# Rotation partners: four SBUF to SBUF transfers in place of a permutation product

## What is computed

```python
def apply_rope_2(x, cos, sin):
    x1, x2 = jnp.split(x32, 2, axis=-1)
    return jnp.concatenate([x1 * c - x2 * s, x2 * c + x1 * s], axis=-1)

def axial_rope_2(x, row_cs, col_cs):
    return jnp.concatenate([apply_rope_2(x[..., :half], *row_cs),
                            apply_rope_2(x[..., half:], *col_cs)], axis=-1)
...
qa = axial_rope_2(rms(qa, q_norm_a[l]), row_cs, col_cs)      # 8 query heads
ka = axial_rope_2(rms(ka, k_norm_a[l]), row_cs, col_cs)      # 2 key heads
y_a = gqa_attention(qa, ka, va) @ w_branch_a[l]
for g in range(3):                                           # 3 dilated groups, 4 heads
    qs.append(apply_rope_2(rms(qb, q_norm_b[l, g]), *seq_cs))
    kss.append(apply_rope_2(rms(kb, k_norm_b[l, g]), *seq_cs))
y_b = dilated_attention(qs, kss, vs) @ w_branch_b[l]
```

## Time and profile before

| | |
|---|---|
| median of 3 runs | 3612.27 us (3611.25 to 3614.24) |
| the profiled execution | 3599.83 us, span 3598.0 us |
| TensorE busy | 3462.9 us, 96% of the span |
| VectorE busy | 2141.8 us, 60% |
| ScalarE busy | 1230.7 us, 34% |
| GpSimd busy | 332.7 us, 9% |
| TensorE's granted clock, mean | 0.988 |
| chain that ended last | TensorE 52%, issue 32%, VectorE 11%, ScalarE 4% |
| DMA | 359.58 MB, mean 100 GB/s |

### The profile page before, as it was taken

One profiled execution on the slowest core, in us unless ns is written; L12 is line 12 of the kernel. 1 busy time (PEld: TensorE's weight loads), 2 busy tenths in 40 slices (PEclk: granted clock), 3 DMA queues, 4 the chain that ended last, 5 costly groups with the idle time before them and its releaser, 6 DMA issues.

```text
span 3598.0 us, 45143 instructions
## 1 busy us (share of the span) xinstructions
PE 3462.9 (96%) x17184; PEld 2724.0 (76%) x17184; DVE 2141.8 (60%) x2850; ACT 1230.7 (34%) x1526; POOL 332.7 (9%) x334
## 2 busy tenths in 40 slices
PE   7999999999999998999998999999999999999999
PEld 3677768888888676678886477878888577878887
DVE  6457558666666465576667566366667665355443
ACT  1235435112213355342225333342223433333222
POOL 0000102001002000010003010011001010001000
PEclk9999999999999998999999999999999999999999
DMA  8221202322232122034442011234443011222222
GB/s 337 82 78 53 75 0 83 128 106 93 97 125 90 57 77 74 21 141 164 163 163 78 31 66 54 88 124 169 163 163 135 32 66 47 82 106 94 93 94 105
DMA packets 52252, 359.58 MB, mean 100 GB/s; under 512 B 5960, under 2 KB 6600, under 8 KB 11024
## 3 DMA queue, kind: packets, MB, share of 16 engines
q1 hardware_dynamic: 35744, 256.92, 20.2%
q10 hardware_dynamic: 16368, 100.73, 7.6%
HBM read 355.31 MB, written 2.32 MB: 99 GB/s over the span
## 4 chain that ended last, share of the span: by engine, by line
PE 52%; issue 32%; DVE 11%; ACT 4%; DMA 1%; POOL 1%; DVEq 0%; ACTq 0%; POOLq 0%
PE pair L548 21%; PE pair L1045 11%; PE pair L616 3%; DVE arena L2190 2%; PE pair L1115 2%; PE pair L586 2%; PE pair L719 1%; PE pair L878 1%; DVE w_lo L2105 1%; PE pair L560 1%; PE pair L967 1%; ACT w_hi L1399 1%; PE pair L1187 1%; PE pair L942 1%; DVE arena L2465 1%
## 5 line engine op out<-in xcount | busy, mean ns | idle before, releaser
L2105 DVE TENSOR_TENSOR w_lo<-raw,w_hi 128x2048 fp32r<-128x2048 f32 x221 | 506.9, 2294 | 263.8 <-ACT w_hi L1399 258.1
L1399 ACT ACTIVATE w_hi<-raw 128x2048 fp32r<-128x2048 f32 x221 | 421.6, 1908 | 661.1 <-PE pair L548 608.5
L548 PE MATMUL pair<-h_hi,w_hi 128*128 128x512 f32 (+2 forms) x1856 | 597.4, 364 | 5.7 <-DVEq L2087 2.7
L548 PE MATMUL pair<-h_hi,w_lo 128*128 128x512 f32 (+2 forms) x1856 | 594.5, 362 | 0.0
L548 PE MATMUL pair<-h_lo,w_hi 128*128 128x512 f32 (+2 forms) x1856 | 594.3, 362 | 0.0
L548 PE MATMUL pair<-u_hi,w_hi 128*128 128x512 f32 (+3 forms) x1152 | 388.4, 373 | 10.2 <-DVE x L2146 5.8
L2190 DVE SCALAR_TENSOR_TENSOR arena<-arena,cact 128x256 f32<-128x256 f32 x756 | 375.7, 520 | 19.5
L548 PE MATMUL pair<-u_hi,w_lo 128*128 128x512 f32 (+3 forms) x1152 | 381.9, 368 | 0.0
L548 PE MATMUL pair<-u_lo,w_hi 128*128 128x512 f32 (+3 forms) x1152 | 381.2, 367 | 0.0
L548 PEld LDWEIGHTS pair<-h_hi,w_hi 128*128 128x128 f32 (+2 forms) x1856 | 309.1, 183 | 67.4 <-issue 7.3
L548 PEld LDWEIGHTS pair<-h_hi,w_lo 128*128 128x128 f32 (+2 forms) x1856 | 308.9, 183 | 62.3
(11 more groups left out here) (359 smaller groups left out, 4961.7 us busy)
## 6 DMA issues: line engine op xcount, KB each, us to landing
raw<-in_wt_dram SPq DMA_DIRECT2D x222, 1024.0 KB, 4.8
arena<-in_modw_dram ACTq DMA_DIRECT2D x78, 1024.0 KB, 4.9
arena<-in_modw_dram SPq DMA_DIRECT2D x18, 1024.0 KB, 7.2
arena<-negm_rows_dram ACTq DMA_DIRECT2D x16, 384.0 KB, 4.3
arena<-in_fconst_dram ACTq DMA_DIRECT2D x2, 2688.0 KB, 9.8
x<-in_xt_dram SPq DMA_DIRECT2D x1, 3072.0 KB, 16.4
arena<-in_brope_dram ACTq DMA_DIRECT2D x4, 640.0 KB, 3.9
out_dram<-x SPq DMA_DIRECT2D x1, 2048.0 KB, 7.2
```

Of the source, the lines that this page charges most:

```text
L548: mm = pe.matmul(pp[p][0:m, lo:hi], a[0:rows, k * width + c0:k * width + c0 + m], b[0:rows, k, lo:hi], start=(k == 0 and i == 0), stop=(k ...
L1399: act.activation(w_hi[slot][:], raw[slot][:], ACT.Copy).then_inc(w_hi_done, 1)
L2105: dve.tensor_tensor(w_lo[slot][:], raw[slot][:], w_hi[slot][:].bitcast(F32), ALU.subtract)\
```

## The change

The permutation product (L1055) is gone. Instead ScalarE, behind the two reads of a rotation, waits for its own scaling and issues four transfers of 32 rows x 512 (64 KB each) from qg to a new buffer qs, which swap the two blocks of 32 rows within each 64. VectorE waits for all four (64 on a semaphore of the rotation's parity) and multiplies qs by the sine from SBUF, where it read bank 3. So that the partner is always 32 rows away, the host puts the columns of the grouped queries and keys, their gains and the tables in another order; the part of the table where the permutation was is loaded as zeros. The scaling signals the semaphore `rope_gained` in place of `act_pool`; GpSimd waits for that.

```diff
+        rope_gained = sem("rope_gained")
+        rope_partner = [sem(f"rope_partner_in{i}") for i in range(2)]
-        b_perm = area(0, P)
+        g_qs = [area(GR0 + 16 * S + i * S, S) for i in range(2)]
+        r_qs = [area(R0 + (13 + i) * S, S) for i in range(2)]
...
-            def bank_rope(slot, sq, qg):
+            def bank_rope(slot, sq):
                 pair_read(slot)
                 take_pair(2)
                 pe.matmul(bank(2), b_blk, sq, start=True, stop=True).then_inc(job_act, 1)
-                take_pair(3)
-                pe.matmul(bank(3), b_perm, qg, start=True, stop=True).then_inc(job_dve, 1)
...
+            def partner(i, qs, qg):
+                act.wait_ge(rope_gained, t.next(rope_gained))
+                for at in range(0, P, 64):
+                    for a, b in ((at, at + 32), (at + 32, at)):
+                        act.dma_start(qs[a:a + 32, :], qg[b:b + 32, :]).then_inc(rope_partner[i], 16)
+
-            def rope_scaled(slot, col, qg, sq):
+            def rope_scaled(slot, col, i, qg, sq, qs):
                 act.wait_ge(rope_done, t.next(rope_done))
-                act.activation(qg, bank(slot), ACT.Copy, scale=prm[:, col:col + 1]).then_inc(act_pool, 1)
+                act.activation(qg, bank(slot), ACT.Copy, scale=prm[:, col:col + 1]).then_inc(rope_gained, 1)
                 act.activation(sq, bank(slot), ACT.Square).then_inc(pair_free[slot], 1)
+                partner(i, qs, qg)
...
-                                   scale=prm[:, col:col + 1]).then_inc(act_pool, 1)
+                                   scale=prm[:, col:col + 1]).then_inc(rope_gained, 1)
                     act.activation(g_sq[i], late_y[i], ACT.Square, bias=bias[:, i, 0:1]).then_inc(pair_free[i], 1)
+                    partner(i, g_qs[i], g_qg[i])
...
-            def bank_rope(tm, qc, root, hi, lo, source, back):
-                job()
-                finish(dve.tensor_tensor(tm, bank(3), b_sin, ALU.mult), pair_free[3])
+            def bank_rope(tm, i, qs, qc, root, hi, lo, source, back):
+                dve.wait_ge(rope_partner[i], t.next(rope_partner[i], 64))
+                finish(dve.tensor_tensor(tm, qs, b_sin, ALU.mult))
...
-                    pool.wait_ge(act_pool, t.next(act_pool))
+                    pool.wait_ge(rope_gained, t.next(rope_gained))
...
-        w = a["w_in_2"][l]
+        w = a["w_in_2"][l][:, _turned_columns()]
...
+def _turned_head():
+    return np.arange(64).reshape(2, 2, 16).transpose(1, 0, 2).reshape(-1)
+
+def _turned_columns():
+    cols = np.arange(768 * 4 + 2048)
+    cols[:640] = (64 * np.arange(10)[:, None] + _turned_head()[None, :]).reshape(-1)
+    return cols
```

More of the change, by code:

```diff
@@ L1124, in gqa @@
                 pe.wait_ge(const_in["gqa"], t.next("gqa", 16))
-                bank_rope(0, g_sq[0], g_qg[0])
+                bank_rope(0, g_sq[0])
                 w = tile()
                 bank_product(w, 0, 256, 0, job_act, h_wait)
-                bank_rope(1, g_sq[1], g_qg[1])
+                bank_rope(1, g_sq[1])
                 bank_product(w, P, 256, 1, tile_used)
-                bank_rope(0, g_sq[0], g_qg[0])
+                bank_rope(0, g_sq[0])
                 t.next(rope_done)
@@ L1271, in dilated @@
                             bank_product(w, (i + 1) % 2 * P, 256, (i + 1) % 2, job_act if i % 2 else tile_used)
-                        bank_rope(i % 2, r_sq[i % 2], r_qg[i % 2])
+                        bank_rope(i % 2, r_sq[i % 2])
                     if pr == 0:
@@ L1855, in scaled @@
                     job(last=last)
-                    rope_scaled(slot, PQA, g_qg[i % 2], g_sq[i % 2])
+                    rope_scaled(slot, PQA, i % 2, g_qg[i % 2], g_sq[i % 2], g_qs[i % 2])
                 def by_feature():
@@ L1916, in project @@
                     job(last=i % 2 == 1)
-                    rope_scaled(i % 2, PQB + i, r_qg[i % 2], r_sq[i % 2])
+                    rope_scaled(i % 2, PQB + i, i % 2, r_qg[i % 2], r_sq[i % 2], r_qs[i % 2])
                 def placed(g, c, heads):
@@ L2643, in rope @@
                     hi, lo = (g_kh, g_kl) if i == 0 else (g_qh[:, i - 1, :], g_ql[:, i - 1, :])
-                    bank_rope(g_tm, g_qc[i % 2], g_r[i % 2], hi, lo, g_tm, hi.bitcast(F32))
+                    bank_rope(g_tm, i % 2, g_qs[i % 2], g_qc[i % 2], g_r[i % 2], hi, lo, g_tm, hi.bitcast(F32))
                 def maxima(j, part=range(NT)):
@@ L2688, in rope @@
                         hi, back, lo = (v.rearrange("p a (b u) -> p a b u", b=2) for v in (hi, back, lo))
-                    bank_rope(r_tm, r_qc[i % 2], r_r[i % 2], hi, lo, source, back)
+                    bank_rope(r_tm, i % 2, r_qs[i % 2], r_qc[i % 2], r_r[i % 2], hi, lo, source, back)
                 def masked(n, b):
@@ L3033, in _weights @@
     return np.stack(tiles + [tiles[0]] * 2)
+def _turned_head():
+    import numpy as np
+    return np.arange(64).reshape(2, 2, 16).transpose(1, 0, 2).reshape(-1)
+def _turned_columns():
+    import numpy as np
+    cols = np.arange(768 * 4 + 2048)
+    cols[:640] = (64 * np.arange(10)[:, None] + _turned_head()[None, :]).reshape(-1)
+    return cols
 def _swap32():
@@ L3082, in _constants @@
     tabs = [
-        (np.concatenate([np.cos(v) for v in (a16[0], a16[0], a16[1], a16[1])]),
-         np.concatenate([-np.sin(a16[0]), np.sin(a16[0]), -np.sin(a16[1]), np.sin(a16[1])]),
-         np.arange(64).reshape(2, 2, 16)[:, ::-1].reshape(-1)),
-        (np.concatenate([np.cos(a32), np.cos(a32)]), np.concatenate([-np.sin(a32), np.sin(a32)]),
-         np.arange(64).reshape(2, 32)[::-1].reshape(-1)),
-    ]
-    for b, (cos, sin, partner) in enumerate(tabs):
-        perm = np.zeros((P, P))
-        for half in range(2):
-            perm[64 * half + partner, 64 * half + np.arange(64)] = 1.0
-        brope[b] = np.concatenate([perm, blk, np.tile(cos, (2, 1)), np.tile(sin, (2, 1))], 1)
+        (np.concatenate([np.cos(a16[0]), np.cos(a16[1]), np.cos(a16[0]), np.cos(a16[1])]),
+         np.concatenate([-np.sin(a16[0]), -np.sin(a16[1]), np.sin(a16[0]), np.sin(a16[1])])),
+        (np.concatenate([np.cos(a32), np.cos(a32)]), np.concatenate([-np.sin(a32), np.sin(a32)])),
+    ]
+    for b, (cos, sin) in enumerate(tabs):
+        brope[b] = np.concatenate([np.zeros((P, P)), blk, np.tile(cos, (2, 1)), np.tile(sin, (2, 1))], 1)
     u = np.arange(P)
@@ L3151, in _pack @@
         else:
-            prm[l, :, PQA] = np.tile(a["q_norm_a_2"][i], 2)
-            prm[l, :, PKA] = np.tile(a["k_norm_a_2"][i], 2)
+            prm[l, :, PQA] = np.tile(a["q_norm_a_2"][i][_turned_head()], 2)
+            prm[l, :, PKA] = np.tile(a["k_norm_a_2"][i][_turned_head()], 2)
             for g in range(3):
```

## The result

The changed kernel takes **3633.4 us** in the median of 4 runs (3631.07 to 3635.45); the kernel before, run beside it, 3612.65 (3611.25 to 3614.24). The ratio is **1.0055, interval 1.004 to 1.0071**: about 20 us slower. The profiled execution took 3631.07 us, span 3629.3.

A forecast was written before the change was run, and what follows sets the result against it. The ScalarE-VectorE chain was to replace TensorE as pacesetter in the rotations; losses of 1.5 + 3.0 (grouped-query), 0.7 + 0 (first halves) and 2.8 + 2.8 (second halves) made 10.8 us, 3612.3 to 3623.1 us; range 3594 to 3636.

The forecast's parts named there:

- no wait for a transfer: Sign in the rotations: VectorE never waits for a transfer; the partner's landing has some 2.4 us of cover.
- the block of four issues: On ScalarE between scaling and root: four issues and a wait hold it 1.95 us, upper bound 2.44.
- Rival C: Transfers landing 3 to 4 us later, or a ScalarE block of 2.4 us: 3629 to 3636 us, chance 0.15.
- The chain's link: Scaling, root and VectorE per rotation: from 5.26 to 6.84 us, more than TensorE's 6.35 without the permutation.
- grouped-query link: Chain per rotation where it ends in u_hi and u_lo: 0.58 us shorter than 6.84, so 6.26 us.
- First halves: First dilated half of each layer: loss about 0.7 us in layer 2, 0 in layer 3.
- Second halves: Second dilated half: loss 2.8 us per layer, 5.6 in two.
- the 0.9 us at rotation 0: Second dilated half: of the root's 1.58 us delay about 0.7 is covered and 0.9 moves rotation 1's end.
- No block at all: All rotation stages, if ScalarE's issues cost nothing: 18.6 us faster, gained only where TensorE sets the pace.
- The transfers at no cost: Rotations: the transfers themselves cost nothing, the fourth landing about 4.4 us after the scaling's start, before VectorE asks at 6.8.
- A: Issues on ScalarE nearly free or beside its work: over 6 us faster, up to 18.6 (3594 us), chance 0.23.
- B: ScalarE's block is 1.5 us, so gain and loss cancel: 3612 us, chance 0.22.

The follow-up runs named there:

- e1: The changed kernel without its four transfers, so neither permutation product nor partner exchange; VectorE multiplies qg itself by the sine: 3604.88 us, ratio 0.9968 to the kernel before.
- e5: As e1, but GpSimd's product by the cosine covers only 32 of 512 columns and VectorE adds qg itself: 3597.69 us, ratio 0.9965.
- e11: The changed kernel with its own four transfers issued by SyncE between weight tiles instead of by ScalarE: 3599.84 us, ratio 0.9964.
- e9: The changed kernel with GpSimd's product by the cosine cut to 32 of 512 columns and VectorE adding qg itself: 3640.24 us, ratio 1.0085.
- e4: The changed kernel with ScalarE taking a rotation's root before issuing the next rotation's four transfers: 3632.36 us, ratio 1.0041.
- e2: The kernel before, permutation product kept, plus the change's four transfers into a buffer nobody reads: 3644.04 us, ratio 1.008.
- e3: The changed kernel with two transfers of every second row instead of four, partners in neighbouring rows: 3622.3 us, ratio 1.0011.
- e6: The changed kernel with one transfer of all 128 rows instead of four, rows not exchanged: 3604.28 us, ratio 0.9974.
- e7: As e3, but GpSimd issues the two transfers ahead of its product by the cosine: 3620.34 us, ratio 1.0024.
- e12: As e11, but GpSimd's product by the cosine is held until VectorE has added the rotation before: 3614.63 us, ratio 1.0007.

## Why the prediction was right, and where it was not

**The mechanism** was right, and all but one of its marks are in the trace. The chain of scaling, root, VectorE and rope_done sets the pace; TensorE stands before its block product; the gain on TensorE is more than given back. The one that failed, no wait for a transfer, is taken up below. Forecast 3623.1, measured 3633.4: inside the range but near its top (3636), and above the forecast's own part of it (3615 to 3629).

**The term that was mis-sized is the block of four issues.** The prediction took 1.95 us "since it is the only row of four issues in sequence" and put the upper bound at 2.44 from "the slowest of the one kind of transfer that leaves SBUF". The block is 3.23 - 0.69 = 2.54 us: 2.46 for the four issues and 0.08 around them, which is above even that bound. The rows of four in sequence were loads of weights and parameters from memory; the row that was nearest in kind, a transfer that starts in SBUF, has 0.57 for one of its two issues and 0.335 for the other, and was used for the bound only. The prediction's own two points, 10.8 us at 1.95 and 23 at 2.44, make 25 us of loss for each us of block; 0.59 more gives 10.8 + 14.7 = 25.5, where the six stages lost 24.3. That this comes so close is partly luck, as the stages below show. Rival C's "block of 2.4" was thus the true case, at a chance of 0.15; its late landings were not (2.0 us).

**The chain's link:** 5.26 + (2.54 - 0.37) = 7.43 by the prediction's steps (0.37 is the 1.06 less the scaling's 0.69), and 7.41 in the trace. The grouped-query link, forecast 6.26, is 6.8 with the longer block.

**The stages** were less well divided than their sum. First halves: 0.7 and 0 forecast, 4.6 and 4.5 measured. The last block product comes 3.5 us later within its stage (2106.10 in the earlier trace rows, 2116.43 now, with 6.8 us between the starts of the stage); the prediction had 1.4, and the longer block adds 4 x 0.59 = 2.4. That makes 3.8. But then the missing permutation should have given 0.85 back, and the stage lost 4.6: from the block product to its end it takes 1.1 us more, not 0.85 less. These 1.9 us are what the rows above give for the lower clock, to which TensorE came back from a gap of 6.2 us. That a lower clock eats such gains was not in the prediction. No run tries it alone. Second halves: 2.8 forecast, 3.3 and 3.7 measured, with the longer block partly offset because the 0.9 us at rotation 0 was hidden entirely: rotation 1 is done at 2204.64, less the 11.4 us by which this stage starts later 2193.24, where it was 2193.55 before. By the prediction's steps the block of 2.54 should have cost 2.8 + 4 x 0.59 = 5.2 in each second half. By the same steps the first halves should have cost 0.7 + 2.4 = 3.1 and 0 + 2.4, and measured 4.6 and 4.5, the clock's part among it. So the second halves came out some 3 us cheaper in sum and the first halves about as much dearer: two misses that cancel in the 25.5.

**No block at all** was put at 18.6 us of gain. e1 had 12.5, and e5 17.5. What lay between these two is a step that the prediction lacks: it moved tm's partner operand from PSUM to SBUF and costed that at nothing. That 17.5 meets the 18.6 is in part luck, since e5 also frees the sums that were longer before. The clock has its part too: in the first half of layer 3 e1 gained 0.7 us at 0.97 and e11 3.9 at 1.00, where the prediction had 4.3. The same place before and after, GpSimd's product with tm starting beside it; before first:

```profile
2199.78 2.47 POOL L2919 TENSOR_TENSOR arena<-arena 128x512 f32<-128x512 f32 x1 [4.17 <-ACT arena L1831]
...
2201.01 0.68 DVE L2632 TENSOR_TENSOR arena<-pair,arena 128x512 f32<-128x512 f32 x1
```

```profile
2212.81 2.67 POOL L2930 TENSOR_TENSOR arena<-arena 128x512 f32<-128x512 f32 x1 [5.61 <-ACT arena L1839]
...
2214.25 1.78 DVE L2643 TENSOR_TENSOR arena<-arena 128x512 f32<-128x512 f32 x1
```

With one operand in PSUM tm takes 0.68 us while GpSimd works, with both in SBUF 1.78. The Trainium skill (SBUF — State Buffer, Who interferes with whom) says that a VectorE instruction with two SBUF inputs contends with a GpSimd instruction that reads SBUF, because its second input comes over a port that the two share; the traces agree. It costs 5 us where the chain on VectorE is what counts (e1 to e5, by the stages of one profile each) and nothing where ScalarE is (e9). The kernel before was not free of it: its sum reads two operands from SBUF as well, and the one at 2194.38 took 1.78 us.

**The transfers at no cost** was right for the landing as such (e11 equals e1, and 2.0 us landing against the forecast 1.8). "No wait of VectorE for a transfer" was not, and it was one of the prediction's own signs of being wrong: there are ten, 20.8 us. But 13.2 of them are ahead of the first rotation of the two second halves, where VectorE stood 9.6 us each for TensorE before; the other eight make 7.6 us, and behind each of the ten VectorE waits another 1.4 to 4.7 us for the root. e4 shows what they cost once that cover is taken away.

**The rule that was weighed.** The issue takes 0.61 us and its data land 2.0 us after it; four issues, 2.45 us, are more than the landing of any one. "Usually small relative to the DMA" (the Trainium skill, DMA: Bandwidth & Descriptors, Issuing engines are not separate DMA queues) does not describe this case, and the prediction was right not to follow it. The other half of the same section, that issuing from another engine saves the sequencer's time and only that, is what e11 shows: the six stages go from +24.3 to -12.5 with the very same transfers.

**Rivals.** A (issues nearly free) falls by e2, B (a block of 1.5) by the trace, D (TensorE's full 29 us) by e1.

## What to carry to other kernels

An issue of a DMA is an instruction of the engine that makes it, about 0.5 to 0.6 us here whether it moved 64 or 256 KB, and it counts as busy nowhere on the page: price it by the nearest kind and by its place in a row of issues (the first of a row is the cheapest), times the number of issues, and put it between the two instructions that it separates. If that is a chain with less slack than that, move the issues to a queue whose engine only waits, before giving up the idea. And when an operand moves from PSUM to SBUF, look up who else reads SBUF at that moment.

## What the runs showed that was not expected

- The issue's time goes by its place in a row of issues more than by its size. On ScalarE the first of four takes 0.51 us in most rotations and the later ones 0.61 (32 rows, 64 KB); the first of e3's two takes 0.47 and the second 0.62 (64 rows, 128 KB); e6's single one 0.47 (128 rows, 256 KB). The load of the mask is the same instruction throughout; here it is alone (before) and then right behind four issues (the change):

```profile
L1974 ACTq DMA_DIRECT2D arena<-in_mask_dram x2: 334/334/334, 2083.6 to 2914.7; - x2
```

```profile
L1984 ACTq DMA_DIRECT2D arena<-in_mask_dram x2: 592/592/592, 2093.5 to 2939.8; - x2
```

- Which of VectorE's instructions gets longer depends on which one GpSimd's product of 1.3 us happens to meet: tm goes from 0.69 to 1.79 us at most, the product by the root from 0.69 to 1.38 (e7), the high part from 0.43 to 1.38 (the median of the 18 in e12 that write u_hi). Holding that product back only chose another victim.
- A gap of 6 us ahead of one block product leaves TensorE at a granted clock of 0.5 to 0.7 for the 10 us around it, and that product and those behind it took about 1.9 us longer: a wait costs more than its length. And the granted clock of a stage differs from one execution to the next by 3 to 5 us of its length, which is as much as several of the steps tried here.
